# Attention keys stored unsplit and split per chunk on the way in; the order of query and value weights and of ScalarE's query splits changed

## What is computed

```
u = rms_norm(h, pre_mix_gain)
proj = u @ w_in
qa, ka, va, qb, kb, vb, g = jnp.split(proj, SPLITS, axis=-1)
qa, ka, qb, kb = rope(...) each
o_swa  = windowed_gqa_sink_attention(qa, ka, va, attn_sink, pos, is_real)   # 16 heads, 4 kv heads, width 64
lam    = exp(sum(lambda_q1 * lambda_k1)) - exp(sum(lambda_q2 * lambda_k2)) + lambda_init
o_diff = differential_attention(qb, kb, vb, lam, ...)                      # 8 heads: softmax(q1 k1) - lam softmax(q2 k2)
gates  = sigmoid(g + b_gate)
merged = g_swa * (o_swa @ w_branch_swa) + g_diff * (o_diff @ w_branch_diff)
h = h + rms_norm(merged @ w_out, post_mix_gain)
```

## Time and profile before

| what | us |
|---|---|
| median of three runs | 875.66 |
| lowest, highest | 875.16, 877.67 |
| the profiled execution, its own time | 876.87 |
| its span, first to last instruction | 875.1 |
| TensorE busy | 862.2 (99%) |
| VectorE busy | 629.0 (72%) |
| ScalarE busy | 468.0 (53%) |
| GpSimd busy | 73.7 (8%) |
| mean granted TensorE clock | 0.999 |

### The profile page before, as it was taken

The page is one execution under the profiler, slowest core; times in us unless marked ns, Lnnn a source line. Parts: engine busy times, 40 slices in busy tenths (PEclk is TensorE's granted clock), DMA queues, the critical chain, the costliest instruction groups (busy, mean ns, idle before and its releaser), DMA issues.

```text
span 875.1 us, 13099 instructions
## 1 busy us (share of the span) xinstructions
PE 862.2 (99%) x4820; PEld 737.9 (84%) x4820; DVE 629.0 (72%) x985; ACT 468.0 (53%) x756; POOL 73.7 (8%) x96
## 2 busy tenths in 40 slices
PE   8999999999999999999999999999999999999997
PEld 6887788888888888889889888788888888888886
DVE  5867677766876666668778887888766876666665
ACT  6546534434644444444566887676653654444443
POOL 1000000000200000002322010133300100000000
PEclk9999999999999999999999999999999999999999
DMA  9955344554565555352798443755474365455531
GB/s 331 400 212 192 116 169 149 192 188 149 186 241 191 192 192 192 144 192 86 259 274 288 136 157 117 246 192 172 169 269 173 122 225 190 177 198 188 189 143 48
DMA packets 31774, 167.21 MB, mean 191 GB/s; under 512 B 4128, under 2 KB 5920, under 8 KB 14320
## 3 DMA queue, kind: packets, MB, share of 16 engines
q1 hardware_dynamic: 28992, 159.17, 51.8%
q10 hardware_dynamic: 2736, 7.42, 2.4%
HBM read 157.02 MB, written 3.83 MB: 184 GB/s over the span
## 4 chain that ended last, share of the span: by engine, by line
PE 86%; DVE 6%; ACT 3%; DMA 1%; issue 1%; POOL 1%; SPq 0%; ACTq 0%; DVEq 0%
PE ps L522 16%; PE ps L524 16%; PE ps L523 16%; PE ps L688 8%; PE ps L673 8%; PE ps L692 4%; PE ps L669 4%; PE ps L701 2%; DVE wlo L1859 2%; ACT whi L862 1%; PE ps L557 1%; PE ps L1755 1%; DMA kswap<-kraw 1%; PE ps L703 1%; PE ps L1713 1%
## 5 line engine op out<-in xcount | busy, mean ns | idle before, releaser
L1859 DVE TENSOR_TENSOR wlo<-raw,whi 128x2048 fp32r<-128x2048 f32 x134 | 307.4, 2295 | 146.3 <-ACT whi L862 145.9
L862 ACT ACTIVATE whi<-raw 128x2048 fp32r<-128x2048 f32 x134 | 256.2, 1913 | 180.0 <-PE ps L524 109.0
L522 PE MATMUL ps<-whi,xT 128*128 128x512 f32 x192 | 76.8, 400 | 0.0
L524 PE MATMUL ps<-whi,xT 128*128 128x512 f32 x192 | 75.0, 391 | 0.0
L523 PE MATMUL ps<-wlo,xT 128*128 128x512 f32 x192 | 74.8, 390 | 0.0
L1326 POOL TENSOR_TENSOR stat<-stat,cst 128x1 f32<-128x1 f32 x10 | 11.9, 1200 | 490.0 <-DVE stat L1879 261.0
L522 PE MATMUL ps<-whi,fT_h 128*128 128x512 f32 x128 | 50.2, 392 | 0.0
L523 PE MATMUL ps<-wlo,fT_h 128*128 128x512 f32 x128 | 49.8, 389 | 0.0
L524 PE MATMUL ps<-whi,fT_l 128*128 128x512 f32 x128 | 49.8, 389 | 0.0
L522 PE MATMUL ps<-x_all,whi 128*128 128x272 f32 x160 | 46.5, 291 | 1.6 <-DVE wlo L1859 1.5
L523 PE MATMUL ps<-x_all,whi 128*128 128x272 f32 x160 | 46.1, 288 | 0.0
(11 more groups left out here) (349 smaller groups left out, 1886.9 us busy)
## 6 DMA issues: line engine op xcount, KB each, us to landing
raw<-weights SPq DMA_DIRECT2D x134, 1024.0 KB, 4.8
kB<-key_parts SPq DMA_DIRECT2D x20, 272.0 KB, 3.5
kswap<-kraw SPq DMA_DIRECT2D x26, 136.0 KB, 2.5
key_parts<-knat SPq DMA_DIRECT2D x4, 544.0 KB, 7.3
cst<-consts SPq DMA_DIRECT2D x1, 1371.0 KB, 13.3
raw<-weights SPq DMA_DIRECT2D x4, 256.0 KB, 5.1
raw<-weights SPq DMA_DIRECT2D x2, 512.0 KB, 6.7
gate_a<-gain_rows ACTq DMA_DIRECT2D x2, 512.0 KB, 7.9
```

The costliest lines, as they stand in the source:

```text
L522: pe.matmul(o, lh, rh, start=first, stop=False)
L524: return pe.matmul(o, ll, rh, start=False, stop=last)
L862: act.activation(whi[s][:], raw[s][:], ACT.Copy).then_inc(split_hi, 1)
L1859: dve.tensor_tensor(wlo[s][:], raw[s][:], whi[s][:], ALU.subtract).then_inc(split_lo, 1)
```

## The change

**Keys.** `keys_high` and the subtraction no longer stand between rotation and store. `store_keys` writes the rotated, unsplit keys from `kswap` (half the bytes), one blob earlier in SP's loop (m = 5 to 9) and at the end of the iteration, ahead of the next weight's load; it waits for `rot_ok`. `swap_halves` now waits until the store of the blob that had the buffer has landed (`kd_out`). `load_keys(e)` fetches an unsplit chunk into a ring `ktwo` of two buffers, and for each of ten chunks ACT makes the high half (`keys_high(e)`) and POOL the low one (`keys_rest(e)`) in `kB`, at the ends of the slots in `KEYS_AT`.

**Queries and values.** Blobs 11 and 12 change their roles: 11 is a query blob, 12 a value blob, and the transposes of the third value blob move from slot 24 to slot 26. `queries_high` moves to the end of its q, behind the exponential and the scaling. POOL's loop is now written slot by slot, with query subtractions, key subtractions and the norms of differential units in one order.

**Others.** The bias rows of the first gate go from ACT at q = 38 to SP's iteration m = 22. `step_lambda` on DVE moves from q = 14 to q = 13.

PE's matrix products are the same ones; those of blobs 11 and 12 and one group of transposes change places.

The diff, cut to its core:

```diff
-QUERIES = (6, 7, 9, 10, 12, 13, 15, 17)
+QUERIES = (6, 7, 9, 10, 11, 13, 15, 17)
-VALUES = (5, 8, 11, 14, 16)
+VALUES = (5, 8, 12, 14, 16)
-VALUES_AT = {12: 0, 18: 1, 24: 2, 30: 3, 34: 4}
+VALUES_AT = {12: 0, 18: 1, 26: 2, 30: 3, 34: 4}
+KEYS_AT = {17: 0, 19: 1, 32: 2, 38: 3, 40: 4, 42: 5, 44: 6, 46: 7, 48: 8, 50: 9}
...
             def swap_halves(m2):
...
-                if swaps_before(m2):
-                    sp.wait_ge(kt_ok, max(SWAPPED.index(m) for m in SWAPPED if m < m2 and m % 2 == b) + 1)
+                last = max((m for m in SWAPPED if m < m2 and m % 2 == b), default=None)
+                if last in QUERIES:
+                    sp.wait_ge(kt_ok, QUERIES.index(last) + 1)
+                elif last is not None:
+                    sp.wait_ge(kd_out[b], stored(last))
...
             def store_keys(i):
-                sp.wait_ge(kt_ok, i + 1)
-                parts = knat[i % 2][:].bitcast(F32)
+                sp.wait_ge(rot_ok, i + 1)
+                v = kswap[i % 2]
...
+            def load_keys(e):
+                i, cc = (0, e) if e < 2 else (e // 2, e % 2)
+                if e == 0:
+                    sp.wait_ge(kd_out[0], stored(4))
+                if e >= 2:
+                    sp.wait_ge(kb_lo, e - 1)
+                for u in range(2):
+                    v = kd[i, u::2, cc].unsqueeze(1).to_broadcast([DH, 2, KEYS])
+                    sp.dma_start(ktwo[e % 2][:, u, :], v).then_inc(ktwo_in[e % 2], 16)
...
                 load(n, w[n], n - 2)
                 m = n - N1
-                if 6 <= m < 11:
-                    store_keys(m - 6)
-                if m in (12, 13):
-                    load_shared_keys(m - 12)
-                if m == 19:
-                    load_keys(0)
-                if 22 <= m < 29:
-                    load_keys(m - 21)
+                if m in (10, 11, 14, 15):
+                    load_keys((10, 11, 14, 15).index(m))
+                if 22 <= m < 28:
+                    load_keys(m - 18)
+                if m == 22:
+                    sp.wait_ge(u_sc, S_UNITS)
+                    for t in range(NT):
+                        sp.dma_start(gate_s[:, t, :], grow[5].partition_broadcast(P)).then_inc(bias_in[2], 16)
                 if m - 7 in QUERIES:
                     store_queries(m - 7)
                 if m - 4 in SWAPPED:
                     swap_halves(m - 4)
+                if 5 <= m < 10:
+                    store_keys(m - 5)
...
-            def keys_high(i):
-                act.wait_ge(rot_ok, i + 1)
...
-                act.activation(knat[i % 2][:, :, 0], kswap[i % 2][:], ACT.Copy).then_inc(rot_hi, 1)
+            def keys_high(e):
+                act.wait_ge(ktwo_in[e % 2], 32 * (e // 2 + 1))
+                if e >= 2:
+                    act.wait_ge(u_sc, sets_read(e))
+                act.activation(kB[e % 2][:, :, 0, :], ktwo[e % 2][:], ACT.Copy).then_inc(kb_hi, 1)
...
-                if q in (4, 6, 8, 10, 12):
-                    keys_high(q // 2 - 2)
-                if q % 2 == 1 and (q - 5) // 2 in QUERIES:
-                    queries_high((q - 5) // 2)
...
-                if q == 38:
-                    act.wait_ge(u_sc, S_UNITS)
-                    bias_rows(2, gate_s)
+                if q % 2 == 1 and (q - 5) // 2 in QUERIES:
+                    queries_high((q - 5) // 2)
+                if q in KEYS_AT:
+                    keys_high(KEYS_AT[q])
...
+            def keys_rest(e):
+                pool.wait_ge(kb_hi, e + 1)
+                pool.tensor_tensor(kB[e % 2][:, :, 1, :], ktwo[e % 2][:], kB[e % 2][:, :, 0, :],
+                                   ALU.subtract).then_inc(kb_lo, 1)
...
-                        pe.wait_ge(kb_in[key_slot(U)], keys_loaded(U))
+                        pe.wait_ge(kb_lo, key_set(U) + 1)
...
-                if q == 14:
+                if q == 13:
                     step_lambda()
```

More of the change, by code:

```diff
@@ L143, in query_of, with key_set, sets_read, stored @@
     return U // S_UNITS * 4 + cc // 2
-def key_slot(U):
+def key_set(U):
     cc, _ = unit_place(U)
[L149 to L155, removed]
+    return cc // 4 if U < S_UNITS else 2 + cc
+def sets_read(e):
+    return 0 if e < 2 else 8 if e == 2 else 2 * e + 10
+def stored(i):
+    return 16 * (i // 2 + 1) + (0 if i % 2 else 32)
 def slot_of(n):
@@ L315, in build @@
         vb_meta = new("vb_meta", [P, D])
+        ql = [at("ql0", [P, 2, TOK], F32R, top[0])]
         top[0] += 1536 - 960
@@ L331, in build @@
         assert dead + KC * TOK + 2 * P <= cst_at + NCONST
-        kd = nc.dram_tensor("key_parts", (5, P, 2, 2, KEYS), F32, kind="Internal").ap()
+        kd = nc.dram_tensor("key_parts", (5, P, 2, KEYS), F32, kind="Internal").ap()
         top[0] = region + NT * D
@@ L1366, in _ @@
                                    ALU.subtract).then_inc(kt_ok, 1)
-            for U in range(S_UNITS, UNITS):
-                pool.wait_ge(d_o, U - S_UNITS + 1)
-                st = ostat[:, U % 3]
-                link(pool, "pool", rsqrt(st[:, 2:3], st[:, 1:2], st[:, 0:1], 1.0 / P))
-                pool.tensor_scalar(o_tok[U % 3][:], o_tok[U % 3][:], st[:, 2:3], None, ALU.mult).then_inc(d_n, 1)
+            def keys_rest(e):
+                pool.wait_ge(kb_hi, e + 1)
+                pool.tensor_tensor(kB[e % 2][:, :, 1, :], ktwo[e % 2][:], kB[e % 2][:, :, 0, :],
+                                   ALU.subtract).then_inc(kb_lo, 1)
+            for q in range(2 * OUT2):
+                if q % 2 == 1 and (q - 5) // 2 in QUERIES:
+                    queries_rest((q - 5) // 2)
+                if q in KEYS_AT:
+                    keys_rest(KEYS_AT[q])
+                U = q - U0 - 3
+                if S_UNITS <= U < UNITS:
+                    pool.wait_ge(d_o, U - S_UNITS + 1)
+                    st = ostat[:, U % 3]
+                    link(pool, "pool", rsqrt(st[:, 2:3], st[:, 1:2], st[:, 0:1], 1.0 / P))
+                    pool.tensor_scalar(o_tok[U % 3][:], o_tok[U % 3][:], st[:, 2:3], None, ALU.mult).then_inc(d_n, 1)
             for t in range(NT):
@@ L1755, in slot @@
                             m = pe.matmul(ps[:, 4 + u, 0:KEYS], qT[u][:, cc, t * P:(t + 1) * P],
-                                          kT[:, 2 * u + v, 0:KEYS].bitcast(F32R), start=v == 0, stop=v == 1)
+                                          kT[:, u, v, :], start=v == 0, stop=v == 1)
                     m.then_inc(u_sc, 1)
```

54 lines of the change are left out of this document (18 added, 36 removed).

## The result

The changed kernel took 878.82 us (median of ten runs, 876.24 to 879.83) against 875.67 for the kernel before (ten runs): a ratio of 1.0029, with a 95% interval of 1.0019 to 1.0038. It became 2.5 us slower by the ratio (3.1 by the medians), where 0.4 faster was forecast. The time lies above the range too. The profiled execution took 879.83 us; its span is 878.0 us and its mean granted clock 0.996, where the one before had 875.1 and 0.999. It is the slowest of the ten, so what follows reads a late execution.

A forecast was written before the change was run, and what follows sets the result against it. TensorE was taken to bound the kernel, with work in 862.2 of 875.1 us. Terms -1.8 - 0.2 + 2.7 - 0.7 - 0.4 = -0.4 gave 876.5 for the profiled execution, 875.3 by the median; range 872.3 to 877.9.

The forecast's parts named there:

- Keys off ScalarE, blob 7: Ahead of query blob 7: without early key splits on ScalarE, the 1.85 us stop mostly goes, 1.6 us gained.
- the low half that was feared as next: VectorE's low half for blob 7, behind key blob 4's rotation, expected late next; 0 to 0.5 us of stop stays.
- Blob 5: Stop at 429.33: swap of key blob 2 lands 0.75 us later, second rotation product 1.18 shorter, so -0.2 us.
- The two ends: Landing of key blob 2's swap: 423.5 at best, 427 at worst; term ahead of blob 5 from -1.7 to +1.9 us.
- swaps land late: Rival: key blob 2's swap behind weight 6's load takes 6.11 us, early gain vanishes; +1.7, 877.4 us, chance 0.1.
- Slots 25 and 26: New 2.5 us stop for the third values' copy behind scaling and query split, with smaller terms +2.7 us.
- Slot 30: Blob 12 no longer a query, so no subtraction delays the scaling and copy; the 0.74 us stop goes, -0.7 us.
- Slot 40: Bias rows leave ScalarE's queue, query subtraction moves, key split comes in; the 0.95 us stop shrinks, -0.4 us.
- Differential units: From slot 42: 2.1 us slack at TensorE's turn covers a key split plus VectorE hold of 1.5 us, so 0.
- The slower rival: Key subtractions hold VectorE in slots 38 to 50, 0.66 to 0.96 us each, 7 times; 880 to 882 us, chance 0.08.

The follow-up runs named there:

- the bias rows' execution: Profiled execution of the changed kernel with the two bias rows issued by ScalarE at q = 38 as before; median 878.18 us, ratio 1.0029.
- the two other orders of SyncE: Changed kernel with key blob 0's store behind weight 6's load: 878.25 us; changed kernel with swap and store ahead of the load at m = 6 to 8: 880.63 us.
- the kernel with the old roles: Changed kernel with blobs 11 and 12 in their old roles and the third values turned in slot 24; 875.48 us, ratio 0.9989.

## Why the prediction was wrong

- **Keys off ScalarE, blob 7: right.** -1.95 against -1.6; the low half that was feared as next ended at 442.10, ahead of TensorE's start on blob 7 at 444.34. It cost nothing either where TensorE came less late from blob 5: in the bias rows' execution it ended at 440.17, 0.75 us ahead of TensorE.
- **Blob 5: the step that failed.** "My estimate is 424.5" for the landing of the swap; it landed at 426.04 and the rotation began at 426.07. The term that was too small is "plus what the 1 MB load in front of them costs". The store that the swap waits for landed at 419.37, even earlier than the forecast 420.5, but the swap's second DMA took 6.06 us. The two ends were 423.5 and 427, and the price of the late end, +1.9, met the measured +1.72, in an execution that was itself a late one. The rival "swaps land late" described it, with 0.1. What spoke against it, "that this swap ran with DMA queues much fuller", does not hold: one 1 MB load in front was enough (6.06 us against the 6.11 of the earlier trace rows, 2.4 of the earlier trace rows); with a load issued only behind it, in the two other orders of SyncE, the same DMA took 2.5 and 2.6 us. The moved load was treated as a cost of the swap only in passing, though a load that is held back meets what is issued behind it.
- **The low clock** was missing as a term: +1.5. The stops of the earlier trace rows, at most 1.70 us, did not show it, and the rival that priced the late swap took TensorE to go on at full speed.
- **Slots 25 and 26: right in place and cause**, 2.17 against 2.7.
- **Slot 30: right in size, wrong in cause.** It goes with blob 12 still a query blob, so the exchange of roles is not needed for it. The forecast was right that the subtraction beside the softmax step made the scaling late (1.25 us, 0.15 in the kernel with the old roles); what moved the subtraction away there is the query splits' new place behind the scaling. That place was not changed back in a run of its own. The exchange brought only the stop in slot 26.
- **Slot 40: half the size, wrong cause in part.** The stop went wholly. The issues of the bias rows alone did not make it. What is left is the query subtraction beside the softmax step, which took 1.06 in the earlier trace rows and 0.22 now. That is read from the traces; no run puts only the subtraction back.
- **Differential units: wrong slack.** The 2.1 us of the earlier trace rows were measured at the turn of the scores. TensorE's products with the values and the scores of the next unit wait too, and in the trace before they had about 1.1 and 0.9 us in the same slots. The split and what follows ate that, where 0 was put down: +1.8. The slower rival had the place and the sign, but not the size: 0.3 to 0.7 us in each of slots 46, 48, 50 and 51, at other waits of TensorE than the one it named.

Without blob 5 and its clock the measured terms add up to 0.0, near the -0.2 that was forecast for them. That is luck: slots 46 to 51 lost about what the other places gained beyond their forecasts.

## What to carry over

A step that is moved ahead of a load moves the load too; ask what is issued behind the load, since a small transfer behind a large one can land as late as the large one does (here 426.04 for the swap and 424.97 for the load). Look for the instruction that passes lateness on, here the low half of a weight behind a rotation that it does not need: turning two instructions round was worth more than the orders of the DMAs that were tried. And measure the slack at every wait of the engine that sets the time, not at one of them in a slot; a stop may cost more than it lasts. And look at more than one execution of the same code before a stop is given a price: the one ahead of blob 5 lasted 2.1 to 3.3 us.

## What the runs showed of the hardware

- TensorE's granted clock went to its lower level for some 3.4 us after it had stood for 3.3 us amid dense work, and not when constants were multiplied through the same stop. The cost was 1.5 us, about half of the stop again. After stops of 1.9 us in slot 26 it fell in three executions of eight.
- The DMAs of a swap, 136 KB each, took 2.2 to 2.6 us with no load in flight and 4.0 to 7.1 when a load of 1 MB had been issued less than 2 us ahead of the swap.
- The wait between VectorE and GpSimd goes both ways. A product of GpSimd that takes 0.61 us alone took 2.14 beside VectorE's low half in the changed kernel (591.74 to 593.88, the low half from 591.09 to 593.39). The Trainium skill says on its page "SBUF — State Buffer", section "Who interferes with whom", that who issues first holds the shared ports, and the other waits. Both holds in this document, 1.15 and 2.14, agree with it.
